# Seams of a two-model stack: the residual updated, transposed and copied by column halves

## The reference

```python
h = h + hybrid_mixer(rmsnorm(h, norm_mix[layer]), ...)
h = h + swiglu(rmsnorm(h, norm_ffn[layer]), w_gate[layer], w_up[layer], w_down[layer])
...
x = x + 0.5 * rms_norm(swiglu_2(rms_norm(x, g[0]), ffn_w_in[i, 0], ffn_w_out[i, 0]), g[1])
hm = rms_norm(x, g[2])
...
x = x + rms_norm(m, g[3])
x = x + 0.5 * rms_norm(swiglu_2(rms_norm(x, g[4]), ffn_w_in[i, 1], ffn_w_out[i, 1]), g[5])
```

## Time and profile before

| | |
|---|---|
| median of 3 runs | 2805.44 us (2801.05 to 2805.73) |
| the profiled execution | 2804.22 us |
| its span | 2802.4 us |
| mean granted TensorE clock | 0.982 |
| TensorE busy (products / weight loads) | 2663.9 us, 95% / 2299.8 us, 82% |
| VectorE, ScalarE, GpSimd busy | 1836.9, 1466.8, 158.6 us |
| instructions | 43798 |
| the seams' transposes, L526 | 256, in 16 seams |
| their copies, L538 | 256, in 16 seams |
| first products, L656 | 768, in 16 seams |

### The profile page before, as it was taken

The page is one execution under the profiler, slowest core; times in us unless marked ns, Lnnn a source line. Parts: engine busy times, 40 slices in busy tenths (PEclk is TensorE's granted clock), DMA queues, the critical chain, the costliest instruction groups (busy, mean ns, idle before and its releaser), DMA issues.

```text
span 2802.4 us, 43798 instructions
## 1 busy us (share of the span) xinstructions
PE 2663.9 (95%) x15490; PEld 2299.8 (82%) x15490; DVE 1836.9 (66%) x2602; ACT 1466.8 (52%) x2331; POOL 158.6 (6%) x231
## 2 busy tenths in 40 slices
PE   6899998999899989999989899999999999999998
PEld 6888887888688868888889588888887888887887
DVE  5766657676576676666675566666656666666666
ACT  3545545455454565455554555554555555455644
POOL 0000000000000030000000300000011000003000
PEclk9999999999999999999998999999999999999999
DMA  4346642466566446656654246666545665653664
GB/s 133 107 145 202 190 122 89 156 186 195 175 180 186 152 129 179 184 164 202 195 167 126 82 131 199 188 177 183 157 132 171 201 197 169 189 165 111 181 188 138
DMA packets 575630, 457.02 MB, mean 163 GB/s; under 512 B 19084, under 2 KB 537764, under 8 KB 575524
## 3 DMA queue, kind: packets, MB, share of 16 engines
q1 hardware_dynamic: 574852, 455.05, 54.0%
q10 hardware_dynamic: 640, 0.52, 0.1%
q0 software_dynamic: 32, 0.02, 0.0%
HBM read 452.37 MB, written 1.07 MB: 162 GB/s over the span
## 4 chain that ended last, share of the span: by engine, by line
PE 67%; issue 13%; DVE 9%; ACT 4%; DVEq 2%; POOL 1%; DMA 1%; SPq 1%; POOLq 0%; ACTq 0%
PE acc L690 17%; PE tp L675 11%; PE gu L675 11%; PE tp L679 6%; PE gu L679 6%; DVE lo_a L440 4%; ACT hi_a L428 2%; PE gu L656 2%; POOL arena L1018 1%; PE tp L1152 1%; PE gu L1201 1%; PE acc L1234 1%; PE gu L1203 1%; PE gu L1202 1%; DVE small L985 1%
## 5 line engine op out<-in xcount | busy, mean ns | idle before, releaser
L440 DVE TENSOR_TENSOR lo_a<-raw_a,hi_a 128x2048 fp32r<-128x2048 f32 (+1 forms) x313 | 711.6, 2273 | 373.2 <-ACT hi_a L428 371.6
L428 ACT ACTIVATE hi_a<-raw_a 128x2048 fp32r<-128x2048 f32 (+1 forms) x313 | 590.7, 1888 | 113.5 <-PE gu L1198 28.8
L675 PE MATMUL tp<-xT,hi_a 128*128 128x512 f32 x1760 | 438.7, 391 | 0.0
L675 PE MATMUL gu<-xT,hi_a 128*128 128x512 f32 x1600 | 397.9, 391 | 0.0
L675 PEld LDWEIGHTS tp<-xT,hi_a 128*128 128x128 f32 x1760 | 322.7, 188 | 62.0
L675 PEld LDWEIGHTS gu<-xT,hi_a 128*128 128x128 f32 x1600 | 294.0, 188 | 56.9
L690 PE MATMUL acc<-hi_b,h_hi 128*128 128x512 f32 x800 | 314.2, 393 | 0.0
L690 PE MATMUL acc<-lo_b,h_hi 128*128 128x512 f32 x800 | 313.7, 392 | 0.0
L690 PE MATMUL acc<-hi_b,h_lo 128*128 128x512 f32 x800 | 311.2, 389 | 0.0
L451 DVE TENSOR_TENSOR lo_b<-raw_b,hi_b 128x1024 fp32r<-128x1024 f32 x220 | 268.0, 1218 | 0.5 <-ACT hi_b L447 0.5
L750 ACT ACTIVATE arena<-arena 128x256 f32<-128x256 f32 x220 | 92.0, 418 | 325.0 <-DVE arena L771 325.0
(11 more groups left out here) (292 smaller groups left out, 4139.7 us busy)
## 6 DMA issues: line engine op xcount, KB each, us to landing
raw_a<-in_ffn_w_in SPq DMA_DIRECT2D x352, 512.0 KB, 5.7
raw_b<-in_ffn_w_out SPq DMA_DIRECT2D x176, 512.0 KB, 3.6
raw_a<-in_w_in SPq DMA_DIRECT2D x52, 512.0 KB, 4.7
raw_a<-in_w_gate SPq DMA_DIRECT2D x44, 512.0 KB, 5.0
raw_a<-in_w_up SPq DMA_DIRECT2D x44, 512.0 KB, 6.1
raw_b<-in_w_down SPq DMA_DIRECT2D x44, 512.0 KB, 3.6
raw_a<-in_w_out SPq DMA_DIRECT2D x24, 512.0 KB, 4.3
raw_a<-in_c_w_in SPq DMA_DIRECT2D x24, 512.0 KB, 4.6
```

Source lines behind the costliest of these rows:

```text
L428: nc.scalar.activation(a_view(hi_a, par)[:, :, 0:width], a_view(raw_a, par)[:, :, 0:width], ACT.Copy).then_inc(a_hi, 1)
L440: nc.vector.tensor_tensor(a_view(lo_a, par)[:, :, 0:width], a_view(raw_a, par)[:, :, 0:width], a_view(hi_a, par)[:, :, 0:width].bitcast(F3 ...
L675: nc.tensor.matmul(banks[:, e, :], w_hi[:, kt, e * P:(e + 1) * P], xT[:, :, kt, :], start=(kt == 0), stop=False)
```

## The change

Everything goes by column halves over both token tiles. The transposed blocks of (t, h) go to bank 2h + t instead of 2t + h. TensorE turns (0,0), (1,0), (0,1); the transposes of (1,1) stand inside `first_products`, behind the first eight products. ScalarE copies in the order (0,0), (1,0), (0,1), (1,1). VectorE, behind an added norm, updates (0,0), then scales tile 1, then updates (1,0), (0,1), (1,1); without an added norm its order stays. The first products go: high by high and low by high over the first half of the contraction, the same over the second half, then high by low. A product's gate on `turn_hi` is counted by `hi_count` for the new order of copies.

```diff
--- before.py
+++ after.py
@@ -458,7 +458,7 @@
                 split(eng, n, 256 if s.kind == "ffn" else slot_words(s, i))
 
 
-        turn_bank = acc[:, :, :].rearrange("p (t h) (k c) -> p t h k c", t=NT, k=4)
+        turn_bank = acc[:, :, :].rearrange("p (h t) (k c) -> p t h k c", t=NT, k=4)
         turn_others = [gu[:, 0, :], gu[:, 1, :], tp[:, 0, :], tp[:, 1, :]]
 
         def turn_y_pe(pe, L):
@@ -515,23 +515,31 @@
                 eng.wait_ge(loaded, 16 * LOADS)
                 eng.wait_ge(setup_dve, 1)
 
+        def turn_half(pe, s, t, h):
+
+            wait_x(pe, s, t, h)
+            for kt in range(4 * h, 4 * h + 4):
+                mm = nc.tensor.transpose(turn_bank[:, t, h, kt % 4, :], x[:, t, kt * P:(kt + 1) * P], ident)
+            mm.then_inc(turned, 1)
+
         def pre_pe(pe, s):
 
-            for t in range(NT):
-                for h in range(2):
-                    wait_x(pe, s, t, h)
-                    if s.k == 0 and t == 0 and h == 0:
-                        pe.wait_ge(bias_row_ready, 1)
-                    for kt in range(4 * h, 4 * h + 4):
-                        mm = nc.tensor.transpose(turn_bank[:, t, h, kt % 4, :], x[:, t, kt * P:(kt + 1) * P], ident)
-                    mm.then_inc(turned, 1)
+            if s.k == 0:
+                pe.wait_ge(bias_row_ready, 1)
+            turn_half(pe, s, 0, 0)
+            turn_half(pe, s, 1, 0)
+            turn_half(pe, s, 0, 1)
+
+        def hi_count(s, kt):
+
+            return 16 * s.pre + 8 * (kt // 4) + 4 + kt % 4 + 1
 
         def pre_act(act, s):
 
             col = pre_col(s)
-            for t in range(NT):
-                for h in range(2):
-                    act.wait_ge(turned, 4 * s.pre + 2 * t + h + 1)
+            for h in range(2):
+                for t in range(NT):
+                    act.wait_ge(turned, 4 * s.pre + 2 * h + t + 1)
                     if t == 0 and h == 0 and s.k == 0:
                         wait_x(act, s, 0, 0)
                     for kt in range(4 * h, 4 * h + 4):
@@ -560,7 +568,7 @@
 
             col = pre_col(s)
             for h in range(2):
-                dve.wait_ge(turn_hi, 16 * s.pre + 8 + 4 * h + 4)
+                dve.wait_ge(turn_hi, hi_count(s, 4 * h + 3))
                 for kt in range(4 * h, 4 * h + 4):
                     ins = nc.vector.scalar_tensor_tensor(by_t(xT_lo[:, kt, :]), turn_bank[:, :, h, kt % 4, :],
                                                          col(kt), by_t(xT_hi[:, kt, :].bitcast(F32)), ALU.mult, ALU.subtract)
@@ -627,34 +635,42 @@
                 return
             e = 4 * s.post
             dve.wait_ge(gain_full, 16 * (s.gain0 + 1))
-            for t in range(NT):
-                dve.wait_ge(post_sq, e + 2 * t + 1)
-                nc.vector.tensor_tensor(half(xn, t, 0), acc[:, 2 * t, :], gain_b[:, 0:512], ALU.mult)
-                dve.wait_ge(post_sq, e + 2 * t + 2)
-                nc.vector.tensor_tensor(half(xn, t, 1), acc[:, 2 * t + 1, :], gain_b[:, 512:1024], ALU.mult)
+
+            def scaled_out(t, c):
+                dve.wait_ge(post_sq, e + 2 * t + c + 1)
+                nc.vector.tensor_tensor(half(xn, t, c), acc[:, 2 * t + c, :], gain_b[:, c * 512:(c + 1) * 512], ALU.mult)
+
+            def added(t, c):
                 dve.wait_ge(rstdy_ready, 2 * s.post + t + 1)
-                dve.drain()
-                for c in range(2):
-                    nc.vector.scalar_tensor_tensor(half(x, t, c), half(xn, t, c), rstdy[:, t:t + 1], half(x, t, c),
-                                                   ALU.mult, ALU.add).then_inc(x_ready[t], 1)
-
-
-
+                nc.vector.scalar_tensor_tensor(half(x, t, c), half(xn, t, c), rstdy[:, t:t + 1], half(x, t, c),
+                                               ALU.mult, ALU.add).then_inc(x_ready[t], 1)
+
+            scaled_out(0, 0)
+            scaled_out(0, 1)
+            dve.drain()
+            added(0, 0)
+            scaled_out(1, 0)
+            scaled_out(1, 1)
+            dve.drain()
+            added(1, 0)
+            added(0, 1)
+            added(1, 1)
 
         def first_products(pe, s, target, w_hi, w_lo):
 
-            for part in range(3):
-                for q in range(2):
-                    if part == 2:
-                        pe.wait_ge(turn_lo, 2 * s.pre + q + 1)
-                    for kt in range(4 * q, 4 * q + 4):
-                        if part == 0:
-                            pe.wait_ge(turn_hi, 16 * s.pre + 8 + kt + 1)
-                        for e in range(2):
-                            w = (w_lo if part == 1 else w_hi)[:, kt, e * P:(e + 1) * P]
-                            o, opens, closes = target(e, part)
-                            mm = nc.tensor.matmul(o, w, (xT_lo if part == 2 else xT_hi)[:, kt, :],
-                                                  start=(opens and part == 0 and kt == 0), stop=(closes and part == 2 and kt == KT - 1))
+            for part, q in ((0, 0), (1, 0), (0, 1), (1, 1), (2, 0), (2, 1)):
+                if part == 2:
+                    pe.wait_ge(turn_lo, 2 * s.pre + q + 1)
+                for kt in range(4 * q, 4 * q + 4):
+                    if part == 0:
+                        pe.wait_ge(turn_hi, hi_count(s, kt))
+                    for e in range(2):
+                        w = (w_lo if part == 1 else w_hi)[:, kt, e * P:(e + 1) * P]
+                        o, opens, closes = target(e, part)
+                        mm = nc.tensor.matmul(o, w, (xT_lo if part == 2 else xT_hi)[:, kt, :],
+                                              start=(opens and part == 0 and kt == 0), stop=(closes and part == 2 and kt == KT - 1))
+                if part == 0 and q == 0:
+                    turn_half(pe, s, 1, 1)
             return mm
 
         def ffn_in_pe(pe, s, n, m, pa, pm, first=False, last=False):
```

## The result

The changed kernel took 2814.94 us (median of five, 2814.81 to 2817.78) against 2805.44 us (five, 2799.68 to 2805.94): ratio 1.005, 95% interval 1.0038 to 1.0062. The size is less sure than the direction: three of the five times before lie at 2805.4 to 2805.9 and two near 2800, so the medians are 9.5 us apart, the means 12.2, and the ratio stands for 14 (10.6 to 17.4). The profiled execution took 2816.5 us, its span is 2814.7, 12.3 more than before. Busy times hardly differ (TensorE 2666.2 us, ScalarE 1468.6); what grew is waiting.

What follows compares the result with a forecast made beforehand. Taken as the bound: TensorE, with each seam's end set by ScalarE's last copy. Added-norm seams 5.2, less 4.0 for earlier clock falls, plus 2.4 for the other seams, plus 7.2 for falls: +10.8, 2815 us, range 2802 to 2823.

Steps and rivals of the forecast that it cites:

- The chain and its place: Seams between stages: ScalarE's last copy, through squares, root, diagonals and low part, sets the end, not TensorE's first product.
- The last copy 0.52 us later at full clock: Seams behind an added norm: ScalarE's last copy, and with it squares, root, diagonals and low part, 0.52 us later.
- Per kind, 0.52 and 0.35: Added-norm seams at full clock: 0.52 us each into and out of a mixer (4.2), 0.35 ffn to ffn (1.0).
- First block, final, start: 2.4: Seams of the start, first block and final norm: together 2.4 us slower, 1.4 of it at the start.
- The clock: six falls at 1.2: Six of eleven added-norm seams: TensorE's clock falls to 1.2 GHz, 1.2 us each, 7.2; bounds 0 and 13.2.
- The sum: Whole kernel: 5.2 - 4.0 + 2.4 + 7.2 = +10.8 us, said as 2815 us.
- The rule on transposes: TensorE's clock gate: transposes don't count as busy, so falls would become rarer, toward the bound of none.
- TensorE's own path decides: Rival, sixteen seams: first products end 0.24 us earlier each (3.8), falls avoided 4.0, so faster, 2797 us; chance 0.10.
- Clock stays up: Rival, added-norm seams: no or one fall of the clock, +3.6 us, about 2809 us; chance 0.22.

Runs made afterwards that it cites:

- e5: Kernel before with ten unread products in TensorE's pause and squares of x over 64 columns instead of 1024 (not the reference's result): 2790.29 us, ratio 0.9962.
- e6: Changed kernel with ten unread products in TensorE's pause and squares of x over 64 columns instead of 1024 (not the reference's result): 2790.64 us, ratio 0.9958.
- e1: Changed kernel with the transposes of (1,1) in front of the first products again: 2808.53 us, ratio 1.0021 to the kernel before.
- e8: Changed kernel with the transposes of (1,1) in front of the first products and ten unread products in TensorE's pause: 2806.13 us, ratio 1.0017.
- e3: Changed kernel with ten unread products in TensorE's pause in the eleven seams behind an added norm: 2808.17 us, ratio 1.0021 to the kernel before.
- e4: Kernel before with the same ten unread products in TensorE's pause, between the transposes of tile 0 and tile 1: 2797.8 us, ratio 0.9983.
- e2: Changed kernel with VectorE's old order of updates behind an added norm: 2824.98 us, ratio 1.0075 to the kernel before.
- e7: e4 with VectorE's second low part ahead of the diagonals in the six mixer stages: 2797.42 us, ratio 0.9981 to the kernel before.

## Why the prediction was right, point by point

- *The chain and its place.* Right at full clock: the earlier trace rows named the wait that ends last, and after the change it is the same wait, 0.48 us later. e5 and e6 show it by taking the chain away. Not right for the falls of the kernel before, where TensorE's own products ended last (shown with e1); since their price was read from the seams whole, the sum didn't suffer.
- *The last copy 0.52 us later at full clock.* Measured 0.48: 0.37 by the order of the copies (e8's last copy ends at 5.93, before's at 5.56), 0.11 by the transposes behind the products. I had given the order 0.3.
- *Per kind, 0.52 and 0.35.* In the profiles at a steady clock (e3 and e4): into a mixer 0.48, out of a mixer 0.49, ffn to ffn 0.45. The last was undersized by 0.1.
- *First block, final, start: 2.4.* Measured 2.4: 1.47 at the start (said 1.4) and 0.88 in the other four (0.97).
- *The clock: six falls at 1.2.* That it was just six is luck in part: the forecast took over the number of before, e1 and e2 had seven, and which seams would fall was not foreseen and can't be from these rows. The size was a little low from a mixer (1.45). For the six as they fell, 4 x 1.42 + 1.16 + 1.24 = 8.1 instead of 7.2. The six of before had cost 3.8, where 4.0 was said (its six readings, as printed, add up to 4.1). That products in the pause do away with the falls is shown by e3 to e8.
- *The sum.* With what was measured for each term: 5.2 - 3.8 + 2.4 + 8.1 = 11.9, and the seams give 11.8.
- *The rule on transposes.* By it (the Trainium skill, TensorE: Matmul & The Clock Gate, Part 4, PE-mode transpose) falls would have become rarer. The traces don't bear that out: six before, six, seven and seven in the three kernels with the new place of the pause (in e2 the pause is longer, 2.04 us, in the change and e1 it isn't). One execution of each kernel doesn't refute it, and ten products in the pause remove the falls under either reading.
- *The rivals.* "TensorE's own path decides" is refuted by e1 for this kernel, and right for a shorter chain in the seams into an ffn (e6). "Clock stays up" was built as e3: 2808, said 2809.

The sum came out at 11.8 for the seams where 10.8 was said, at 9.5 in the medians and at 12.2 in the means. That the median came so near to the 2815 that was said is luck too: the kernel before alone ranged from 2795 to 2812 us over the two groups.

e4 and e7 are the fastest kernels that keep the whole computation: their medians are 4.5 us under that of the one before, and by their ratios to it (0.9983 and 0.9981 against 1.005) they are 0.7% under the changed one.

## What to carry to other kernels

Before bringing an engine's first work forward, look which chain ends the seam: an earlier start on an engine that nobody waits for pays nothing, and what is put in front of the last input of the real chain is paid in full. Count the items that follow the last ready input in each queue, before and after: eight copies became twelve. Where an engine with a variable clock stands in front of a serial chain, its slow stretch enters the chain, as with the eight products ahead of the last transposes here. Filling its pause with products that nobody reads gained 4.5 us where the reordering lost some ten.

## What the runs showed of the hardware

In e7 a VectorE operation with two inputs in SBUF (L440, 2.28 us) held GpSimd up until its end: a one-column operation of GpSimd that started 0.40 us behind it took 1.96 us instead of 0.23 and ended 0.08 behind it. The Trainium skill (GPSIMD Engine Reference, Key points) says that the two share their SBUF interfaces and contend when VectorE reads two SBUF inputs; the trace agrees, and shows the wait last until VectorE's instruction is through.

With ten products of 256 columns, 1.44 us, in a pause of 1.37 us the granted clock stayed at 2.4 GHz in all eleven seams of both kernels, where six had fallen to 1.2; they delayed the next transposes by nothing that can be seen.
